# Meta tokens' down products with low and high input parts side by side, and attention scores of 64 rows with a head's keys split over two halves of the rows

## What is computed

```python
def dsa_attention(q, k, v, q_idx, k_idx, w_idx, topk):
    ...                                   # token indexer picks topk keys of a query
    logits = jnp.einsum('bqhd,bqkhd->bhqk', qb, k_sel) * scale   # 8 heads of 64
    ...                                   # ALiBi, softmax, times the selected values
def swiglu(h, w_gate, w_up, w_down):
    return (jax.nn.silu(h @ w_gate) * (h @ w_up)) @ w_down       # D_FF = 2816
for layer in range(DEPTH):                # DEPTH = 2
    if layer % 2 == 0:
        mix = attn_recurrent_mixer(...)   # dsa_attention beside HGRN2, then w_out
    else:
        mix = multiscale_pool(h, w_pool[j], pool_scale[j])
    h = layer_norm(ALPHA * h + mix, ln_mix_g[layer], ln_mix_b[layer])
    h = layer_norm(ALPHA * h + swiglu(h, ...), ln_ffn_g[layer], ln_ffn_b[layer])
return h[:, N_META:]                      # the meta tokens are dropped at the end
```

## Time and profile before

| | us |
|---|---|
| three runs before: median (lowest to highest) | 2578.8 (2577.88 to 2579.78) |
| the profiled execution: its own time | 2572.35 |
| its span, first to last instruction | 2570.6 |
| PE busy | 2484.9 (97%) |
| PEld, DVE, ACT, POOL busy | 2136.2, 1288.5, 846.6, 1064.9 |
| mean granted TensorE clock | 0.99 |
| projection, mixers, trunk: about | 465, 488, 1615 |

### The profile page before, as it was taken

One profiled execution on the slowest core, in us unless ns is written; L12 is line 12 of the kernel. 1 busy time (PEld: TensorE's weight loads), 2 busy tenths in 40 slices (PEclk: granted clock), 3 DMA queues, 4 the chain that ended last, 5 costly groups with the idle time before them and its releaser, 6 DMA issues.

```text
span 2570.6 us, 36247 instructions
## 1 busy us (share of the span) xinstructions
PE 2484.9 (97%) x14088; PEld 2136.2 (83%) x14088; DVE 1288.5 (50%) x2467; ACT 846.6 (33%) x1394; POOL 1064.9 (41%) x622
## 2 busy tenths in 40 slices
PE   7999999889999989999999999999999999999997
PEld 7889999668888778898898888888888888888885
DVE  6799999797886433333333433323223332232224
ACT  3684222333443223222222323322333332332222
POOL 1433213454544424444344544444444444454442
PEclk9999999899999999999999999999999999999998
DMA  4101230333333234332232323332333233334331
GB/s 138 34 18 59 79 100 22 107 111 107 103 101 102 87 102 122 97 99 81 84 99 82 92 73 99 93 107 82 96 92 91 81 115 98 89 92 115 109 97 48
DMA packets 274997, 231.39 MB, mean 90 GB/s; under 512 B 10768, under 2 KB 255568, under 8 KB 274832
## 3 DMA queue, kind: packets, MB, share of 16 engines
q1 hardware_dynamic: 266640, 220.59, 28.8%
q10 hardware_dynamic: 8192, 8.52, 0.9%
HBM read 215.81 MB, written 12.71 MB: 89 GB/s over the span
## 4 chain that ended last, share of the span: by engine, by line
PE 59%; DMA 1%; POOL 1%; DVE 0%; ACT 0%; issue 0%; POOLq 0%; SPq 0%; ACTq 0%; DVEq 0%
PE banks L2013 37%; PE banks L2029 20%; PE banks L2065 1%; PE banks L2043 1%; PE banks L2052 1%; DMA cq_raw<-in_w_up 0%; PE banks L1715 0%; DMA last_draw<-in_w_down 0%; POOL dL L1931 0%; POOL wL L1920 0%; POOL wL L1924 0%; DVE y L2233 0%; ACT dH L2115 0%; DVE n_bn L1624 0%; ACT L2124 0%
## 5 line engine op out<-in xcount | busy, mean ns | idle before, releaser
L1924 POOL TENSOR_TENSOR wL<-cq_raw,wH 128x2048 fp32r<-128x2048 f32 x87 | 405.8, 4665 | 529.9 <-ACT wH L2109 529.9
L2013 PE MATMUL banks<-hL,wH 128*128 128x512 f32 (+1 forms) x1760 | 618.3, 351 | 5.0 <-ACT hid L2124 4.8
L2013 PE MATMUL banks<-hH,wL 128*128 128x512 f32 (+1 forms) x1760 | 617.3, 351 | 0.0
L2013 PE MATMUL banks<-hH,wH 128*128 128x512 f32 (+1 forms) x1760 | 615.4, 350 | 0.0
L2213 DVE TENSOR_TENSOR hid<-hid,banks 128x512 f32<-128x512 f32 (+1 forms) x110 | 64.4, 585 | 739.1 <-PE banks L2013 632.2
L2013 PEld LDWEIGHTS banks<-hL,wH 128*128 128x128 f32 x1760 | 330.6, 188 | 54.2 <-ACT hid L2124 5.9
L2013 PEld LDWEIGHTS banks<-hH,wL 128*128 128x128 f32 x1760 | 330.5, 188 | 46.4
L2013 PEld LDWEIGHTS banks<-hH,wH 128*128 128x128 f32 x1760 | 331.1, 188 | 44.9
L1931 POOL TENSOR_TENSOR dL<-last_draw,dH 128x1024 fp32r<-128x1024 f32 x88 | 220.9, 2510 | 332.0 <-ACT dH L2115 331.9
L2233 DVE TENSOR_TENSOR y<-y,banks 128x512 f32<-128x512 f32 (+1 forms) x340 | 233.1, 686 | 203.2 <-PE banks L2029 202.2
L2029 PE MATMUL banks<-dH,hidL 128*128 128x512 f32 (+1 forms) x748 | 296.4, 396 | 2.3 <-issue 2.3
(11 more groups left out here) (257 smaller groups left out, 4224.9 us busy)
## 6 DMA issues: line engine op xcount, KB each, us to landing
cq_raw<-in_w_gate SPq DMA_DIRECT2D x88, 512.0 KB, 4.7
cq_raw<-in_w_up SPq DMA_DIRECT2D x88, 512.0 KB, 5.9
last_draw<-in_w_down SPq DMA_DIRECT2D x88, 512.0 KB, 3.4
w_out_part<-in_w_out SPq DMA_DIRECT2D x60, 512.0 KB, 4.0
va<-in_w_in SPq DMA_DIRECT2D x10, 1024.0 KB, 5.4
va<-in_x SPq DMA_DIRECT2D x8, 512.0 KB, 4.3
vg_scratch<-y ACTq DMA_DIRECT2D x32, 128.0 KB, 1.7
y<-in_x SPq DMA_DIRECT2D x8, 512.0 KB, 7.4
```

The lines of the kernel that those rows point to most:

```text
L1924: nc.gpsimd.tensor_tensor(wL[:, ff % 2, :, :, :].rearrange("p g k f -> p (g k f)"), raw[:, :, :, :].rearrange("p g k f -> p (g k f)"), wH[ ...
L2013: last = nc.tensor.matmul(banks[:, GU + (2 * q + g) % 3, 0:n], wt[:, ff % 2, g, k, :], h[:, k, a:a + n], start=(k == 0 and part == 0), sto ...
```

## The change

Two edits that do not touch each other.

**Meta tokens in the down product.** A new tile `meta_hid` has 48 columns: the low part of the 16 tokens in columns 0 to 15, zeros, the high part in 32 to 47. One matmul of it with `dH` gives low by high in PSUM rows 0 to 15 and high by high in rows 32 to 47; high by low stays a matmul of 16 columns. For each half of D and pair, 6 matmuls become 4. y of tile 0 gathers both parts in two row groups (DVE's add has 48 rows), and `fold` sums them once, after phase 0, with four float32 matmuls by the identity, from which DVE copies the sum back. ACT and DVE write `meta_hid` with one small instruction each per D_FF tile.

**Scores of 64 rows.** `kaT` now holds each head by itself: keys below 512 in rows 0 to 63, those from 512 on in rows 64 to 127. `qaT` holds a head's query in both halves, with no zeros. Each score matmul contracts over 64 rows, the first chunk in one half, the second in the other. The ka units have 512, 264 and 264 tokens in place of thirds, and two copies of 64 rows each; `qa` leaves its bank with four copies in place of two.

```diff
-                kaT = sb(mixer, "kaT", [P, 4, L])
+                kaT = sb(mixer, "kaT", [P, A_HEADS, L - KEY_SPLIT])
...
+def key_rows(a):
+    return (slice(0, HD), 0) if a < KEY_SPLIT else (slice(HD, P), KEY_SPLIT)
...
-            slab_units += [(j, fm, dest, ft, a, n) for ft in range(SW // P) for a, n in CHUNKS3]
+            slab_units += [(j, fm, dest, ft, a, n) for ft in range(SW // P)
+                           for a, n in (((0, KEY_SPLIT), (KEY_SPLIT, 264), (KEY_SPLIT + 264, 264)) if dest == "ka" else CHUNKS3)]
...
-                nc.scalar.activation(kaT[:, half * SW // P + idx, a:a + n], banks[:, bank, 0:n], ACT.Copy)\
-                  .then_inc(slab_out, 1)
+                to, base = key_rows(a)
+                for par in range(2):
+                    last = nc.scalar.activation(kaT[to, 2 * (half * SW // P + idx) + par, a - base:a - base + n],
+                                                banks[HD * par:HD * (par + 1), bank, 0:n], ACT.Copy)
+                last.then_inc(slab_out, 1)
...
+        linked(nc.vector.memset(y[:, 0, :], 0.0))
...
-            return nc.tensor.matmul(logits[0:n, at:at + kn], qaT[:, m % 2, h, 0:n], kaT[:, h // 2, a:a + kn],
+            r, base = key_rows(a)
+            return nc.tensor.matmul(logits[0:n, at:at + kn], qaT[r, m % 2, h, 0:n], kaT[r, h, a - base:a - base + kn],
                                     start=True, stop=True)
...
-                for par in range(2):
-                    r = slice(HD * par, HD * (par + 1))
-                    to = qaT[r, m % 2, :, 0:n].rearrange("p (f two) t -> p two f t", two=2)[:, par]
-                    ins_ = nc.scalar.activation(to, four(src)[r, :, 0:n], ACT.Copy)
+                for half in range(2):
+                    for par in range(2):
+                        to = qaT[HD * half:HD * (half + 1), m % 2, :, 0:n].rearrange("p (f two) t -> p two f t", two=2)[:, par]
+                        ins_ = nc.scalar.activation(to, four(src)[HD * par:HD * (par + 1), :, 0:n], ACT.Copy)
...
-        nc.vector.memset(qaT[:], 0.0).then_inc(dve_pads, 1)
...
+    MH, MB = 32, 32 + N_META
+    meta_hid = sb(c, "meta_hid", [P, 3, MB], F32R)
...
+                if ph.tiles[j // 2] == 0:
+                    at = slice(j % 2 * 512, (j % 2 + 1) * 512)
+                    for u, part in ((0, 0), (0, 1), (1, 1), (1, 0)):
+                        s = (2 * g + u) % 3
+                        if part == 0:
+                            last = nc.tensor.matmul(banks[0:MB, DN + num % 3, :], meta_hid[:, s, :], dH[:, u, at],
+                                                    start=(u == 0), stop=(u == 1))
+                        else:
+                            nc.tensor.matmul(banks[0:N_META, DN + num % 3, :], hidH[:, s, 0:N_META], dL[:, u, at],
+                                             start=False, stop=False)
+                    last.then_inc(down_psum, 1)
+                    continue
...
+        def fold():
+            pe.wait_ge(y_added, downs_to(PAIRS - 2) + 2)
+            for r in (slice(0, N_META), slice(MH, MB)):
+                if r.start:
+                    pe.wait_ge(folded, 1)
+                for half in range(2):
+                    last = nc.tensor.matmul(banks[0:N_META, PB + half, :], ident[r, r], y[r, 0, half * 512:(half + 1) * 512],
+                                            start=(r.start == 0), stop=(r.start > 0))
+                last.then_inc(folded, 1)
...
+                    nc.scalar.activation(meta_hid[:, ff % 3, MH:MB], hid[:, q % 2, 0:N_META], ACT.Copy).then_inc(meta_hi, 1)
...
+                    nc.vector.tensor_tensor(meta_hid[:, ff % 3, 0:N_META], hid[:, q % 2, 0:N_META],
+                                            hidH[:, ff % 3, 0:N_META].bitcast(F32), ALU.subtract).then_inc(meta_lo, 1)
...
-            n = TILES[m][1]
+            n = TILES[m][1] if m else MB
...
+        nc.vector.memset(meta_hid[:, :, :].bitcast(F32), 0.0)
+        nc.vector.memset(y[MH:2 * MH, 0, :], 0.0).then_inc(meta_zero, 1)
...
+                if g == PAIRS:
+                    dve.wait_ge(folded, 2)
+                    for half in range(2):
+                        nc.vector.tensor_copy(y[0:N_META, 0, half * 512:(half + 1) * 512], banks[0:N_META, PB + half, :])\
+                          .then_inc(unfolded, 1)
+                    dve.wait_ge(unfolded, 2)
```

More of the change, by code:

```diff
@@ L60 @@
 LEVELS = 7
+KEY_SPLIT = 512
+def key_rows(a):
+    return (slice(0, HD), 0) if a < KEY_SPLIT else (slice(HD, P), KEY_SPLIT)
 SLOPES = [2.0 ** (-8.0 * (h + 1) / A_HEADS) for h in range(A_HEADS)]
@@ L185, in projection @@
     qi_raw = y[:, 2, :].rearrange("p (a f t) -> p a f t", a=2, f=4)
-    top8 = sb(c, "top8", [P, NT, 8])
+    top8 = squares[:, 0:NT * 8].rearrange("p (m e) -> p m e", m=NT)
     mark = sb(c, "round_mark", [P, 2])
@@ L1365, in off_shared @@
             if what == "qa":
-                if m == 0:
-                    act.wait_ge(dve_pads, 2)
-                for par in range(2):
-                    r = slice(HD * par, HD * (par + 1))
-                    to = qaT[r, m % 2, :, 0:n].rearrange("p (f two) t -> p two f t", two=2)[:, par]
-                    ins_ = nc.scalar.activation(to, four(src)[r, :, 0:n], ACT.Copy)
+                for half in range(2):
+                    for par in range(2):
+                        to = qaT[HD * half:HD * (half + 1), m % 2, :, 0:n].rearrange("p (f two) t -> p two f t", two=2)[:, par]
+                        ins_ = nc.scalar.activation(to, four(src)[HD * par:HD * (par + 1), :, 0:n], ACT.Copy)
             if what == "meta":
@@ L1510, in scores_of @@
             else:
-                dve.wait_ge(dve_pads, 3)
+                dve.wait_ge(dve_pads, 2)
             if h == 0:
@@ L1800, in trunk @@
     stored, gain_kept = sem("stored"), sem("gain_kept")
+    meta_zero, meta_hi, meta_lo, folded, unfolded = (sem("meta_hid_zero"), sem("meta_hi"), sem("meta_lo"), sem("meta_folded"),
+                                                     sem("meta_fold_kept"))
     gain_bank = banks[:, PB:PB + 2, :].rearrange("p b f -> p (b f)")
@@ L2021, in down @@
             pe.wait_ge(hid_lo, units_to(2 * g + 1))
+            if ph.nth == 0:
+                pe.wait_ge(meta_hi, 2 * g + 2)
+                pe.wait_ge(meta_lo, 2 * g + 2)
             for j in range(ph.NJ):
@@ L2089, in _ @@
                     mixes[0] += 1
+            if g == PAIRS:
+                fold()
             gate_up(2 * g + 1)
@@ L2127, in gated @@
                   .then_inc(hid_hi, 1)
+                if a == 0:
+                    if ff == 0:
+                        act.wait_ge(meta_zero, 1)
+                    nc.scalar.activation(meta_hid[:, ff % 3, MH:MB], hid[:, q % 2, 0:N_META], ACT.Copy).then_inc(meta_hi, 1)
         def turned_d(j):
@@ L2216, in gated @@
                 at = slice(a - ph.t0, a - ph.t0 + n)
+                if a == 0:
+                    if ff == 0:
+                        dve.wait_ge(meta_zero, 1)
+                    nc.vector.tensor_tensor(meta_hid[:, ff % 3, 0:N_META], hid[:, q % 2, 0:N_META],
+                                            hidH[:, ff % 3, 0:N_META].bitcast(F32), ALU.subtract).then_inc(meta_lo, 1)
+                    dve.wait_ge(meta_hi, ff + 1)
                 nc.vector.tensor_tensor(hidL[:, ff % 3, at], hid[:, q % 2, 0:n],
```

## The result

The changed kernel takes 2579.9 us (median of 20 runs, 2574.4 to 2588.5) against 2575.7 us for the kernel before (median of 20 runs of it, 2569.1 to 2581.1): a ratio of **1.0021**, 95% interval 1.0013 to 1.003, so **5.4 us slower** (the means differ by 5.4 us, the medians by 4.2). The forecast was 6.0 us faster. The profiled execution took 2580.08 us with a span of 2578.2, 7.6 us more than the span of before.

The account below looks back on a forecast made before the run. PE, busy 97% of the span, was taken to bound the kernel. Terms -6.1 (meta and fold) - 18.2 + 17.0 + 0.8 + 0.5 gave -6.0 us: 2578.8 to 2572.8 us, range 2565.5 to 2583.5.

Parts of the forecast that it names:

- A: Scores: passes start in program order, so half of the 18.2 us gain is lost; +9.1, 2581.9 us; chance 0.10.
- D: Tiles 1 to 3 and 8: no waits cover the row switches; +10.3, so +4.3, 2583.1 us; chance 0.05.
- E: Meta down products: changes of columns cost as changes of rows do; +8.8, so +2.8, 2581.6 us; chance 0.04.
- meta downs, 44 products: Trunk: four matmuls saved for each of 11 pairs, 0.231 us each, all on the path; 10.2 us less.
- fold: After phase 0: eight float32 passes 3.4 us, wait and semaphore 0.25, two row switches 0.39; 4.1 us more.
- nine tiles of `mixers` (-18.2 + 17.0 + 0.8): Scores: overlapping halves save 18.2 us, row switches cost 17.0, ACT's extra `qa` copies 0.8 in tiles 0 to 2.
- `projection`: Key copies of 64 rows give ACT 5.4 us more, mostly absorbed by relu buffers; 0 to 2.5, taken as 0.5.
- B: Scores in tiles 4 to 8: the halves do not overlap at all; +12.2, 2591.0 us, slower; chance 0.08.
- The price of a switch of rows: Scores: 128 to 64 rows costs 0.20 us, back 0.19 (0.15 before transposes), together 0.39 a step; 17.0 us in all.
- the cover: Existing PE waits hide row switches, mainly in tiles 1 to 3 and 8; 17.0 us cost, 27.3 with none.
- Tile 8: Scores: overlap saves 6.9 us, switches cost 2.4, partly hidden in the wait for the maximum; shorter by 4.5 us.
- Rival C: Tiles 1 to 3: changed waits move half-clock stretches; one fewer -11.1, 2567.7 us, chance 0.13; one more -0.9, 2577.9, chance 0.10.

Follow-up runs that it names:

- experiments 2 to 5: On the kernel before: meta part 0.9994, split keys 1.0022, key chunks and copies 1.0018, meta part with VectorE fold 0.9969; changed kernel, tile 5 scores twice: 0.9994.
- the scores part alone: Kernel before with the split keys only (64-row scores, the keys' and queries' copies), trunk as before: ratio 1.0022, 2583.7 us.
- its repeat: Changed kernel with the scores of tile 5 at head 1 issued twice, same result: ratio 0.9994 to the kernel before.
- the copies alone: Kernel before with two key copies of 64 partitions in place of one of 128 in the projection, chunks as before: ratio 1.001.
- both edits: Kernel before with key chunks of 512, 264, 264 tokens and two copies of 64 partitions per bank, scores and trunk as before: ratio 1.0018.

## Why the prediction was wrong, by its own steps

2579.9 us lies inside the stated range of 2565.5 to 2583.5, and that is luck. The forecast stood on a median of 2578.8 before, where twenty runs gave 2575.7; 5.4 us more than 2578.8 would be outside. And the rivals that reached up to there, A, D and E, are not what happened.

The middle column is on record, the right one comes from the segments and experiments 2 to 5. For tiles 2, 3 and 5 the segments compared are without a stretch in either trace: tile 2 of the scores part alone (45.7) against before (45.1), tile 3 of the changed kernel (47.8) against the kernel with the fold on VectorE and the scores of before (49.0), tile 5 with its repeat (53.4) against before (52.9).

| Term | forecast, us | measured, us |
|---|---|---|
| meta downs, 44 products | -10.2 | -9.4 (8.5 in phase 0, 0.9 in phase 1) |
| fold | +4.1 | +7.1 |
| nine tiles of `mixers` (-18.2 + 17.0 + 0.8) | -0.4 | -4.3 at equal clock |
| clock in tile 5 | not in the sum | +6.6 |
| `projection` | +0.5 | +5.9 (3.4 work, 1.7 clock, 0.8 there before the first key copy) |
| sum | -6.0 | +5.9 (all executions: +5.4) |

**Right.** The meta products: 0.23 us apart whatever the columns, so rival E is out, and each pair of D_FF tiles is 0.9 us shorter. (PE is not without a gap in `trunk`, as I wrote: it waits some 5 us in phase 0, before and after alike.) The halves overlap in full, second chunk under the first, so A and B are out: 1.06 us in tile 8, where A wanted 1.39 and B 1.82. The Trainium skill has matmuls strictly first in, first out, in start and end (TensorE: Matmul & The Clock Gate, Part 3, The mechanism). The trace does not agree: in tile 5 two passes of `gram` start at 683.64, ahead of the last pass of the `qk` before it at 683.82. Tiles 6 and 7 were forecast at -0.9 and -2.7 and measured -0.8 and -2.9; tiles 4 and 5 at +1.3 and +0.6, measured +1.0 and +0.4 (the latter with its repeat).

**The price of a switch of rows** was taken too high: 0.39 a visit, where it is 0.28. The 0.20 taken for the way in is right as a sum (0.09 on the way in and 0.10 between the pairs of passes); the way back is 0.09 and not 0.19, and behind `qk_rest` 0.08 and not 0.15. With it went part of the cost at tiles 0 and 1 (forecast +1.5 together, measured +0.7) and at tile 2 (forecast +1.5, measured +0.5), and all of it at tile 3 (forecast +2.0, measured -1.2), where the cover was taken too small as well: PE waits 1.8 us there in the changed kernel and 4.2 in the kernel with the fold on VectorE and the scores of before. That error was in the change's favour.

**Tile 8** gave 2.0 us and not 4.5. Of the difference 0.8 is only where the tile is cut: from its first `gram` on, it lacks its own first `qk`, and from that `qk` on it is 2.8 us shorter. Eight heads gained 0.66 - 0.09 each on the way through `qk` and lost 0.08 behind `qk_rest`, which makes 3.9. But PE then waited for the maximum longer: 5.8 us over 8 against 5.1, this row of the changed kernel:

```profile
PE banks L1198 <- DVE nmax L1460: 5.8, 8, 1.5
```

That leaves 3.2, and 0.4 us are not located.

**The projection** was the first step that failed. The sum charged 5.4 us of ACT with "DVE waits for ACT's relu 8.3 us there, and four relu buffers lie between, so most is absorbed". The row pointed the other way: DVE waiting for ACT means that ACT is late already. Of some 5.4 us more of ACT 2.0 came through with the copies alone, 2.6 with both edits and about 3.4 in the full change, beyond my upper end of 2.5. So the buffers absorb a part, but not most of it. The other 2.5 of the 5.9 were not in the sum at all: 0.8 was there before the first key copy, where two traces of the same kernel differ by 0.3 too, and some 1.7 is the stretch at 139.9. Five of the seven traces of kernels with two copies a bank have a stretch between 137 and 151 us, and none of the nine others has one there.

**The fold** was the second. Its passes were sized nearly right, 4.1 against 3.7 at full clock. I costed what they do and not what they leave behind: 6.8 us at half clock, 3.4 us lost.

**The clock in tile 5** was the third and largest. Rival C had the mechanism, one stretch more or fewer behind a wait, but looked for it in tiles 1 to 3, where waits are long, and gave one stretch more only 5.1 us and a chance of 0.10. In tile 5 the shortened scores lengthened a wait from 0.74 to 1.06 us. I counted this wait as one that gives 0.8 us back, which is right, and not as a place where a shorter product can cost 6.6.

**The clock between the projection and the first `gram`**, +1.7 us in the table of stages, is not in the sum. All eleven traces of kernels in which anything ahead of that place is changed, be it only the chunks or the memset of y, have a stretch of 3.4 or 6.8 us there; the five in which nothing is changed up to there have none. So it comes with the change, and how stays open.

## What to carry to other kernels

Before you shorten work that stands ahead of a wait, ask what the engine gains: if it only waits longer, the best case is nothing and the worst is its clock, and here throwing work away (0.9 us of repeated products) bought back 6.6 us. A small reduction or fold on a few rows belongs on an engine that is idle there. A wait of a consumer for an in-order producer is not cover for more work on the producer: it says that the producer is late already, and here 2.0 to 3.4 of 5.4 us put on it came through. Before you compare two traces at one place, look how far apart they already were ahead of the edit.

## What the runs showed of the hardware that I had not expected

- Eight passes of 16 rows by 16 columns, back to back (PE busy 3.34 of 3.4 us), were followed by 6.8, 6.8 and 3.4 us at 1.2 GHz in the three traces that had them, and by none in the four with the fold on VectorE. Busy time alone does not keep the clock.
- In tile 5 a rest of 1.06 us behind products of 64 rows was followed by 13.7 us at half clock in both traces that had it; rests of 0.74, 0.98, 1.17 and 1.41 us behind products of 128 rows were not (the last three in one trace each).
- Two streams of 512 columns from the two halves of the rows into two banks run side by side: 1.06 us with the switch out, against 1.72 for the same columns one after the other. Passes of the next product of 64 rows can start before the last of them (683.64 against 683.82).
- A switch of rows costs 0.09 us on the way in and 0.08 to 0.09 on the way out, before transposes and products alike; 0.10 more lie between the first and the second pass of each half (0.53 in place of 0.43). A switch between 48 and 16 columns costs nothing.
- The same kernel's profiled executions had spans of 2570.6 and 2577.1 us. The difference is where the stretches at half clock fell. A segment is compared only after the clock of both has been read.
